# The down projection's right low parts: from POOL to DVE, one per step

## What is computed

```python
def ffn_sublayer(h, prev, g, w_gu, conv_w, conv_b, w_down):
    gate, up = jnp.split(rms_norm(h, g) @ w_gu, 2, axis=-1)
    gate_c, state = causal_dwconv3(gate, prev, conv_w)
    return h + (jax.nn.silu(gate_c + conv_b) * up) @ w_down, state
```

## Time and profile before

| What | Value |
|---|---|
| median of 3 runs | 1804.8 us (1800.81 to 1808.76) |
| the profiled execution: time | 1806.58 us |
| the profiled execution: span | 1804.7 us |
| PE busy | 1656.3 us, 92% |
| DVE busy | 1265.1 us, 70% |
| ACT busy | 860.1 us, 48% |
| POOL busy | 839.8 us, 47% |
| mean granted clock of PE | 0.948 of full |

### The profile page before, as it was taken

One profiled execution on the slowest core, in us unless ns is written; L12 is line 12 of the kernel. 1 busy time (PEld: TensorE's weight loads), 2 busy tenths in 40 slices (PEclk: granted clock), 3 DMA queues, 4 the chain that ended last, 5 costly groups with the idle time before them and its releaser, 6 DMA issues.

```text
span 1804.7 us, 32368 instructions
## 1 busy us (share of the span) xinstructions
PE 1656.3 (92%) x12855; PEld 1064.2 (59%) x12855; DVE 1265.1 (70%) x2048; ACT 860.1 (48%) x1610; POOL 839.8 (47%) x780
## 2 busy tenths in 40 slices
PE   6999999988676889989978899899999999989999
PEld 3644444444444656445568754688888888744444
DVE  5856665788697875359655417878878878886592
ACT  5455578754633774442256415544544544443240
POOL 3232266888541110478022425655566666645450
PEclk9998999999877999989978899899999999999999
DMA  7031112112334110467154311212112112244322
GB/s 236 11 110 56 36 36 70 48 70 94 122 117 143 54 48 1 156 228 255 36 164 145 126 30 71 71 49 70 48 48 71 48 48 71 99 138 149 109 88 73
DMA packets 140192, 164.38 MB, mean 91 GB/s; under 512 B 16062, under 2 KB 90878, under 8 KB 140004
## 3 DMA queue, kind: packets, MB, share of 16 engines
q1 hardware_dynamic: 129994, 150.52, 26.1%
q10 hardware_dynamic: 10048, 11.80, 1.9%
HBM read 134.77 MB, written 27.52 MB: 90 GB/s over the span
## 4 chain that ended last, share of the span: by engine, by line
PE 65%; DVE 20%; ACT 7%; issue 4%; POOL 2%; DMA 2%; ACTq 0%; SPq 0%; DVEq 0%
PE PS L1737 23%; PE PS L1798 3%; PE PS L1801 3%; PE PS L1800 3%; PE PS L1084 3%; PE PS L1085 3%; PE PS L1086 3%; ACT arena L1852 2%; ACT arena L1913 2%; PE PS L1279 2%; PE PS L1281 2%; PE PS L1280 2%; PE PS L1437 2%; PE PS L1449 1%; DVE arena L453 1%
## 5 line engine op out<-in xcount | busy, mean ns | idle before, releaser
L1737 PE MATMUL PS<-arena 128*128 128x272 f16 (+1 forms) x3696 | 430.0, 280 | 5.0 <-issue 5.0
L1737 PEld LDWEIGHTS PS<-arena 128*128 128x128 f16 (+1 forms) x3696 | 362.3, 98 | 72.8 <-issue 5.4
L1852 ACT ACTIVATE arena<-arena 128x512 f16<-128x512 f32 (+5 forms) x289 | 167.6, 607 | 250.0 <-PE PS L1737 113.9
L1852 ACT ACTIVATE arena<-PS 128x512 f16<-128x512 f32 (+10 forms) x354 | 175.2, 524 | 174.6 <-PE PS L1449 41.9
L389 POOL TENSOR_TENSOR arena<-arena 128x512 bf16<-128x512 f32 (+2 forms) x144 | 160.3, 1147 | 144.6 <-ACT arena L380 144.3
L1084 PE MATMUL PS<-arena 128*128 128x512 f16 (+2 forms) x584 | 204.3, 361 | 5.9 <-POOL arena L389 4.0
L1085 PE MATMUL PS<-arena 128*128 128x512 f16 (+2 forms) x584 | 203.9, 360 | 0.0
L1086 PE MATMUL PS<-arena 128*128 128x512 bf16 (+2 forms) x584 | 203.7, 360 | 0.0
L3312 POOL TENSOR_TENSOR arena<-arena 128x512 bf16<-128x512 f32 x110 | 127.0, 1158 | 44.4 <-ACT arena L1852 44.4
L1798 PE MATMUL PS<-arena 128*128 128x512 f16 x308 | 116.8, 379 | 1.8 <-POOL arena L1062 1.8
L1801 PE MATMUL PS<-arena 128*128 128x512 bf16 x308 | 116.8, 379 | 0.0
(11 more groups left out here) (379 smaller groups left out, 3868.6 us busy)
## 6 DMA issues: line engine op xcount, KB each, us to landing
arena<-w_gu SPq DMA_DIRECT2D x44, 512.0 KB, 4.6
arena<-w_down SPq DMA_DIRECT2D x22, 512.0 KB, 5.1
arena<-tw_scratch SPq DMA_DIRECT2D x33, 256.0 KB, 2.9
arena<-w_in SPq DMA_DIRECT2D x8, 1024.0 KB, 5.3
arena<-w_kv_mem SPq DMA_DIRECT2D x8, 1024.0 KB, 7.6
arena<-cache_mem_k SPq DMA_DIRECT2D x32, 256.0 KB, 3.3
tw_scratch<-arena SPq DMA_DIRECT2D x7, 1024.0 KB, 4.5
arena<-cache_mem_v ACTq DMA_DIRECT2D x28, 256.0 KB, 4.4
```

Of the source, the lines that this page charges most:

```text
L1737: mm = e.matmul(PS[:, product_bank(f, i) + c, 0:TC], w[:, i, k], s[i][:, q, c, :], start=first, stop=last)
L1852: e.activation(out, in_, ACT.Copy, **kw).then_inc(sem(name), 1)
```

## The change

`right_lo` is defined in DVE's program and no longer in POOL's. DVE calls it once in each step k of each window, behind the step's left sum and the low part of the sum before, and ahead of the window's last low part and of the additions. POOL has no work left in the stage. The operation, its operands, what it waits for (`ws_hi`) and what it signals (`ws_lo`) are the same.

```diff
+            def right_lo(i, k):
+                x = PIECES.index((i, k))
+                e.wait_ge(sem("ws_hi"), upto("ws_hi", x + 1))
+                e.tensor_tensor(z_lo[i % 2][:, k, :], piece(i, k), z_hi[i % 2][:, k, :], ALU.subtract
+                                ).then_inc(sem("ws_lo"), 1)
+
...
                         left_sum(n)
                         if n > first or w in (2, 4):
                             make_left_low(e, n - 1)
+                    right_lo(w + 1, k)
                     if k == KH - 1 and w in (0, 2, 4, 5):
                         make_left_low(e, STEP_ENDS[w + 1] - 1)
                     if w > 0 and k in (4, 7, 9):
...
             down_lo(e, 1, "dw_lo")
 
-            def right_lo(i, k):
...
-            for w in range(6):
-                for k in range(KH):
-                    right_lo(w + 1, k)
-
```

## The result

The changed kernel takes 1808.72 us in the median of 20 runs (1805.85 to 1820.05), the kernel before 1805.43 in 20 of its own (1796.77 to 1808.76). The ratio of the two is 1.004, with a 95% interval of 1.0025 to 1.0054: slower by 7 us (4.5 to 9.7). The two medians differ by 3.3 only, because the times of both kernels lie in two groups: before, eight up to 1800.8 and twelve from 1804.8 on; changed, eleven up to 1809.9 and nine from 1811.6 on. The median of before falls into its upper group and that of the changed kernel on the edge of its lower one. Group for group the means are 1799.5 and 1806.9, then 1806.5 and 1815.0, so 7.3 and 8.5 apart; over all runs they are 1803.7 and 1810.5, 6.8 apart.

A forecast was written before the change was run, and what follows sets the result against it. The prediction took TensorE's matmuls to bound the kernel, with DVE deciding in window 0 and in windows 4 and 5. It summed 4.7 + 2.6 + 1.0 = +8.3 us to a median near 1813.1 us, range 1807.5 to 1819.

The forecast's parts named there:

- The bound and the places: TensorE's matmuls are 84% of the chain; DVE's time in window 0 and in windows 4 and 5 decides.
- The step: Each DVE step with a sum holds a round trip to ACT: 3.24 us instead of 2.89 in window 0.
- Window 0: Eleven longer steps make PE start P1's samples later, at 1618.1 instead of 1613.41: +4.7 us (4.2 to 5.6).
- The stall at ACT's residual loads: Window 0, step k=2: six residual loads on ACT delay DVE by 0.5 us (0 to 1.4).
- The samples' clock: PE's clock in P1's samples after window 0's wait: low either way, put at 0, some 0.5 to either side.
- Windows 1 to 3: The low parts come in time for PE there, 7 us to spare in window 1: no cost.
- Windows 4 and 5: DVE runs out of room; P3's samples wait for the last right low part: +2.6 us (1.4 to 4.4).
- The clock at P3: PE's clock may fall after the new wait at P3's samples: 1.0 us taken out of 0 to 1.7.
- The sum: Whole kernel: 4.7 + 2.6 + 1.0 = +8.3 us, a median near 1813.1 us.
- The freed port pays: Rival: right_lo never waits, steps of window 0 take 2.53 us, 4.0 us less, 1800.8 us; chance 0.05.
- Only window 0 costs: Rival: P3's last low part comes in time, no end wait or clock loss; +4.7, 1809.5 us; chance 0.08.
- The double end: Rival: steps of 3.4 us, P3 waits about 5, clock lost, P7 waits a little; +13, 1818 us; chance 0.09.

The follow-up runs named there:

- e7: The kernel of e1 with ACT's last copy of the states in window 0 moved ahead of step k=9; 0.9947 of the kernel before.
- e8: The kernel before, low parts on POOL, with ACT's last copy of the states in window 0 moved ahead of k=9; 0.9946 of the kernel before.
- e3: The changed kernel with the change in windows 0 to 3 only, POOL making the right low parts in windows 4 and 5; 1.0034 of the kernel before.
- e4: The changed kernel with the change in windows 4 and 5 only, POOL making the right low parts in windows 0 to 3; 1.0024 of the kernel before.
- e5: The changed kernel with each left and right high copy of the stage made by ACT in four parts; 1.0139 of the kernel before.
- e10: The changed kernel run again, nothing altered; 1.0029 of the kernel before, stage 227.1 us.
- e1: The changed kernel with each right low part made one step later on DVE, the last at the window's end; 0.9971 of the kernel before.
- e9: The changed kernel with ACT's last copy of the states in window 0 moved ahead of k=8; 0.9983 of the kernel before.

## Why the prediction was right

**The bound and the places.** Both were the right ones. Window 0's DVE chain moved PE one for one, through ACT's last copy of the states (e7 and e8), windows 4 and 5 ran out of room at P3's samples, and nowhere else did PE wait. e3 and e4 show each alone.

**The step.** Worked out 3.24, measured 3.23, with 0.61 of idle where 0.65 was said. The sum held to its terms: a hand-over from ACT to DVE that no row of before showed was taken as 0.04, and it is that: in the changed kernel ACT's right copy of the step shown above ends at 1597.77, and the right_lo starts at 1597.81:

```profile
1597.16 0.61 ACT L1852 ACTIVATE arena<-turns 128x512 f16<-128x512 f32 x1
```

And e5 shows that ACT's time enters the step whole (0.55 more of copies, 0.56 more of step). The reading of a semaphore that the Trainium skill gives with 50 to 100 ns (Advanced Engine Details and Errata, "Network/Comms") does not appear as a cost of that size at the hand-over: two of 0.08 would have made 3.32 of 3.24, and the trace has 3.23.

**Window 0.** +4.7 was forecast, +4.9 measured (+36.4 against +31.5). The stall at ACT's residual loads was put at 0.5 and was 0.7: the right_lo at k=2 waited 1.3 instead of 0.61. (The first one waited 1.3 too, but it has no left low part ahead of it, and its step took 3.30.) The samples' clock was put at no difference, within 0.5 to either side; it was 0.9 in this execution, outside that, and 0.0 in e10.

**Windows 1 to 3.** Nothing, as said; e3 has no other wait of PE.

**Windows 4 and 5.** +2.6 was forecast. PE's idle time is 2.50, and the wait made the samples of P3 2.7 longer. The last right low part starts at +198.2.

**The clock at P3.** I took 1.0 of 0 to 1.7. It is 1.6 in one execution of the changed kernel and 0 in the other and in e4, after waits that agree to 0.06 us. So a value in the middle was never right as a case, and that it lies near the mean of two executions is luck: I had reasoned from the length of the wait, and the length does not decide. The first stretch of the earlier trace rows also ends 0.1 us after its wait, so it does not show the clock behind it; in the same trace it was 1.00 there too (1579 to 1581).

**The sum.** +8.3 forecast; +10.1 and +7.5 in the two profiled stages; 1.004 (1.0025 to 1.0054) and 1.0029 (1.0007 to 1.005) over all runs, which are +7.2 and +5.2. The median, 1808.7, lies 4.4 under the forecast's 1813.1 and only 1.2 above the lower end of the range. No term of the sum is off by that much. The median of before falls into its upper group of times and that of the changed kernel into its lower one, and between like groups the change adds 7.3 and 8.5, near the +8.3; with one run more in the upper group and one fewer in the lower the median would have come out at 1810.7. The groups go with PE's clock: in the changed kernel the eleven shorter runs have a mean granted clock of 0.949 to 0.953 and the nine longer ones 0.943 to 0.947. What sets it in a run is open. 2.6 us between two executions is the clock in the stage; what lies ahead of the stage was not looked into.

**The rivals.** The freed port pays: this needs the wait gone, and e1 then gives 4.1 less for the stage, where the rival said 4.0. (Its turning point was put at a round trip of 0.96; by the sum of the step it is 2.89 - 0.72 - 0.69 - 0.60 = 0.88. Both lie under the 1.23 of the rows.) The rule behind it is right, that the port which VectorE and GpSimd share is "an exclusive lock" (the Trainium skill, SBUF — State Buffer, "SBUF: two separate sides"): with POOL out of the stage no DVE operation takes 1.57, and the step of the same four operations is 2.53 where three of them beside POOL's took 2.89. It decided nothing in the changed kernel, since the wait took back more. "Only window 0 costs" did not happen. The double end is near e5's case: with 0.56 more in a step P7 waits too.

## What to carry to other kernels

When an operation moves onto an engine that also feeds the one it waits for, ask what stands between its input's request and itself in the queue: here the freed port was worth 0.36 us a step, and a wait of 0.61 in the same step turned that into a loss, while the same operation one step later kept the gain. Before a faster engine is sought for a chain, look at what the waiting engine really waits for: PE's 7.33 us here was for a copy that stood last in ACT's queue for no need, and moving it gave more in the stage than either choice of engine. And compare two profiles over the changed stage, not over the span, where the untouched part differs by more than the effect.

## What the runs showed of the hardware that I had not expected

A part of the program that is the same in all kernels ended between 1571.2 and 1581.9 us in twelve profiled executions, a spread of 10.7 us, more than any effect measured here but e5's; in the two shown above the mean granted clock of PE over it was 0.94 and 0.95.

Splitting a 128x512 copy on ACT into four of 128x128 raises two copies from 1.15 to 1.70 us, so a part of a quarter's size costs 0.21 from start to start and not a quarter of 0.53.

After a wait of PE of 2.5 us at the same place the clock stayed up twice (e4, e10) and fell twice (the changed kernel, e9); the length of the wait alone doesn't tell which.
